# A two-layer hybrid encoder trunk: the streamed tile of the matmuls is read, and PSUM written, from the last column to the first

## The chip, the cores and the metric

The kernel runs on one core of one Trainium2 chip. The metric is device time in microseconds, the median of the runs of one kernel. "The span" is the time from the first to the last instruction of one profiled execution.

## What is computed

The reference is a trunk of two layers over x of 512 tokens by 2048 features, all in fp32. Cut to what matters:

```python
# layer 0
h = rmsnorm(x, a_norm);  proj = h @ a_w_in          # 2048 -> 2 x 2560
xb, gate = proj halves
xb = causal_depthwise_conv(xb)                      # width 4
r = sigmoid(block_diag(xb, w_r) + b_r); i = sigmoid(block_diag(xb, w_i) + b_i)   # 10 blocks of 256
log_a = -8 * r * softplus(-lam); a = exp(log_a)
y = scan(h = a * h + sqrt(1 - a*a) * i * xb)        # along the tokens
x = x + (y * silu(gate)) @ a_w_out                  # 2560 -> 2048
kv = rmsnorm(x, kv_norm) @ w_kv                     # 2048 -> 2 x 2048
# layer 1
proj = rmsnorm(x, b_norm) @ b_w_in                  # q and gate, 2048 each
o = stick_breaking_attention(q, k, v)               # 16 heads of 128, strictly causal
x = x + (o * silu(gate)) @ b_w_out
out = rmsnorm(x, final_norm)
```

## The kernel before

**Two parts for every operand.** TensorE works on fp32r tiles, a rounded form of fp32. To keep the accuracy, each operand is held as a high part (rounded) and a low part (the rest), and each product is three matmuls: high by high, high by low, low by high. `product` (line 355) issues them, and its one `pe.matmul` at line 359 is the line of nearly all matmuls in the profile. They add up in PSUM.

**Weights as the stationary side.** Activations are kept turned: features on the 128 partitions, the 512 tokens along the free axis. In most projections the weight block of 128 by 128 is the stationary operand and the turned activation tile, 128 by 512, is streamed; the result, 128 output features by 512 tokens, fills one PSUM bank of 512 fp32 words. That is `unit_t` (line 363): one unit is one loaded weight tile of 128 by 512, that is two blocks of rows by two blocks of columns, so four products, twelve matmuls, into two banks. `unit_t` is called by `unit1` (line 400, phase 1: the input projection from `x_hi`/`x_lo`, and the two gate matrices of the recurrence from `xc_hi`/`xc_lo`), in the loop of phase 2 (line 442: the output projection from `y_hi`/`y_lo`) and by `proj3` for j under 24 (line 448, phase 3: gate, q and k from `x_hi`/`x_lo`).

**The other matmuls.** In `proj3` from j = 24 on, v is computed with the activations as the stationary side and 256 weight columns streamed. `scores` and `values` do the attention, `turn_weights` (line 480) and `turn_x` (line 388) turn tiles with an identity, `unit4` and `last_columns` do the last projection with the attention output as the stationary side and 512 or 256 weight columns streamed, `add_x1` (line 535) adds the residual by a transpose, and `spread` (line 395) spreads the norm's factors over the partitions: a matmul on plain fp32 tiles, which the engine runs as two passes.

**What sets the order.** Weight tiles arrive from HBM through a ring of four stage slots. SyncE's queue loads a slot once its low part has been made (`lo_ready`). ScalarE makes the high part `w_hi` (lines 593 to 597) when the load has landed and TensorE has finished the unit that used the slot (`w_used`), VectorE makes the low part `w_lo` (lines 838 to 843), and TensorE waits for it at the head of each unit. The readers of the PSUM banks (VectorE, ScalarE) wait for `w_used` of the unit that ends a group; the semaphore is set by the last matmul of the unit. Their work is put by hand at fixed positions between the weight splits. GpSimd makes some of the low parts and masks. VectorE's cumulated products of the attention (line 1047) are scans that read and write `keep` and read `masked` from the last element to the first, and the scan of the recurrence (line 980) runs forward.

Phase 1 has 180 units, phase 2 has 80, and phase 3 has 256, of which 192 go through `unit_t`; the last projection has 64.

Of the kernel before, what the change touches and what calls it, by code (L numbers as in the profile page):

```python
# [32 lines left out]
P = 128  # L33
# [52 lines left out]
def build(nc, x, a_norm, a_w_in, a_conv_w, a_conv_b, a_w_r, a_b_r, a_w_i, a_b_i, a_lambda, a_w_out,  # L86
          kv_norm, w_kv, b_norm, b_w_in, b_w_out, final_norm, out):
    with ExitStack() as ctx:
        def sb(name, shape, dt=F32, scope=ctx):
            return scope.enter_context(nc.sbuf_tensor(name, shape, dt))  # L90
# [22 lines left out]
        w_hi = sb("w_hi", [P, RING, 512], F32R)  # L113
        w_lo = sb("w_lo", [P, RING, 512], F32R)
# [50 lines left out]
        ps = [ctx.enter_context(nc.psum_tensor(f"ps{b}", [P, S], F32)) for b in range(8)]  # L165
# [189 lines left out]
        def _(pe):  # L355
            def product(dst, a_hi, a_lo, b_hi, b_lo, start, stop, check=True):

                for n, (a, b) in enumerate(((a_hi, b_hi), (a_hi, b_lo), (a_lo, b_hi))):
                    mm = pe.matmul(dst, a, b, start=start and n == 0, stop=stop and n == 2,  # L359
                                   skip_group_check=not check)  # L360
                return mm

            def unit_t(j, u, bank, m_hi, m_lo, k0, k_end):

                pe.wait_ge(lo_ready, u + 1)
                s = j % RING
                for kk in range(2):
                    for m in range(2):
                        c = 256 * kk + P * m
                        mm = product(ps[bank + m][:, :], w_hi[:, s, c:c + P], w_lo[:, s, c:c + P],  # L370
                                     m_hi[:, k0 + kk, :], m_lo[:, k0 + kk, :],
                                     k0 + kk == 0, k0 + kk == k_end - 1)
                mm.then_inc(w_used, 1)

# [25 lines left out]
            def unit1(it, j):  # L400

                u = it * N1 + (U1 + j)
                b, jj = j // 18, j % 18
                if jj < 16:
                    unit_t(j, u, 2 * (jj // 8), x_hi, x_lo, 2 * (jj % 8), KD)
                else:
                    if jj == 16:
                        pe.wait_ge(xc_lo_ready, it * 4 + (2 * b + 2))
                    unit_t(j, u, 4 + 2 * (jj - 16), xc_hi, xc_lo, 0, 2)
# [27 lines left out]
            with pe.Fori(0, B2) as it:  # L437
                for j in range(N2):
                    jj = j % 10
                    if j < 10:  # L440
                        pe.wait_ge(y_lo_ready, 1 + 2 * jj + 2)
                    unit_t(j, it * N2 + (U2 + j), 2 * (j // 10), y_hi, y_lo, 2 * jj, KR)
# [53 lines left out]
            for j in range(TURN):  # L496
                if j < 8:
                    pe.wait_ge(x1_lo_ready, 2 * j + 2)
                if j == 6:

                    pe.wait_ge(acc_step, 2 + KD)
                    for t in range(TT):
                        mm = pe.matmul(ps[5][:, t:t + 1], acc[:, P * t:P * t + P], ones[:, 0:1],
                                       start=True, stop=True)
# [748 lines left out]
```

## Time and profile before

| what | value |
|---|---|
| median of 2 runs | 1705.97 us (1705.64 to 1706.29) |
| the profiled execution's own time | 1707.84 us |
| its span | 1706.1 us |
| TensorE busy | 1691.7 us (99%) |
| VectorE, ScalarE, GpSimd busy | 909.6, 798.0, 228.2 us |
| mean granted TensorE clock | 0.998 |
| DMA over the span | 95 GB/s |

PE is TensorE's matmul side and PEld its weight load, DVE is VectorE, ACT ScalarE, POOL GpSimd, SP SyncE. L359 is line 359 of the kernel. In a group, "ps<-x_hi,w_lo" names the output and the inputs, "128x512" the shape of the result, "x1408" the count, and behind the bar stand the busy time in us, the mean duration of one in ns, and the idle time of the engine before them with what ended it. A matmul's duration runs from its start to its modelled end, and those of neighbours overlap.

### The profile page before, as it was taken

To read this page: it belongs to the slowest core of one execution; us is meant where nothing else is said; L and a number is where in the kernel's file an instruction comes from. 1 tells how busy PE (TensorE), PEld (TensorE's weight loads), DVE (VectorE), ACT (ScalarE), POOL (GpSimd) and SP (SyncE) were. 2 spreads that over 40 slices of the span, in tenths; PEclk is the share of its full clock that TensorE was granted. 3 is DMA by queue.
4 is the path that set the end of the run, shared out by engine and by line. 5 is a ranking of instruction groups with operands and counts; after the bars stand their busy time and mean duration, and the time that the engine had idled before them with its cause. 6 is when DMAs were issued, how large, how long until landed. Compare 5 with 4: busy or idle time off the path is not lost.

```text
span 1706.1 us, 25540 instructions
## 1 busy us (share of the span) xinstructions
PE 1691.7 (99%) x8607; PEld 1448.8 (85%) x8607; DVE 909.6 (53%) x1688; ACT 798.0 (47%) x1622; POOL 228.2 (13%) x219
## 2 busy tenths in 40 slices
PE   8999999999999999999999999999999999999998
PEld 7888888888888888888889898988989898898888
DVE  5667676666675344354546455554645455453323
ACT  7655566666555233244445444453444444432223
POOL 0121221212212011021101010111101011112100
PEclk9999999999999999999999999999999999999999
DMA  5333333333333223223232322223232232323223
GB/s 182 99 105 94 98 97 93 91 98 97 100 99 99 94 97 98 92 89 98 75 98 79 90 83 86 86 80 92 81 92 80 86 92 75 98 74 112 93 94 135
DMA packets 155910, 162.22 MB, mean 95 GB/s; under 512 B 9608, under 2 KB 147032, under 8 KB 155736
## 3 DMA queue, kind: packets, MB, share of 16 engines
q1 hardware_dynamic: 155864, 161.63, 30.8%
q8 instruction: 26, 0.43, 0.1%
q14 instruction: 20, 0.16, 0.0%
HBM read 157.39 MB, written 4.19 MB: 95 GB/s over the span
## 4 chain that ended last, share of the span: by engine, by line
PE 98%; ACT 1%; DVE 0%; DMA 0%; issue 0%; POOL 0%; SPq 0%; POOLq 0%; DVEq 0%; ACTq 0%
PE ps L359 96%; PE ps L480 1%; PE ps L388 0%; PE ps L535 0%; DMA xraw<-in_x 0%; DVE rbuf L980 0%; POOL y_lo L1172 0%; ACT w_hi L593 0%; PE ps L395 0%; ACT abuf L677 0%; DVE w_lo L838 0%; DVE tbuf L976 0%; ACT L677 0%; ACT rbuf L665 0%; ACT tbuf L674 0%
## 5 line engine op out<-in xcount | busy, mean ns | idle before, releaser
L359 PE MATMUL ps<-x_hi,w_hi 128*128 128x512 f32 x1408 | 551.7, 392 | 0.0
L359 PE MATMUL ps<-x_hi,w_lo 128*128 128x512 f32 x1408 | 548.8, 390 | 0.0
L359 PE MATMUL ps<-x_lo,w_hi 128*128 128x512 f32 x1408 | 548.7, 390 | 0.0
L841 DVE SCALAR_TENSOR_TENSOR w_lo<-stage,cT,w_hi 128x256 fp32r<-128x256 f32 x416 | 230.5, 554 | 502.2 <-ACT w_hi L597 501.5
L595 ACT ACTIVATE w_hi<-stage,cT 128x256 fp32r<-128x256 f32 x416 | 211.1, 507 | 485.1 <-PE ps L359 484.9
L359 PEld LDWEIGHTS ps<-x_hi,w_lo 128*128 128x128 f32 x1408 | 264.7, 188 | 55.2
L359 PEld LDWEIGHTS ps<-x_hi,w_hi 128*128 128x128 f32 x1408 | 264.9, 188 | 54.5 <-issue 0.7
L359 PEld LDWEIGHTS ps<-x_lo,w_hi 128*128 128x128 f32 x1408 | 265.0, 188 | 54.4 <-issue 0.5
L838 DVE TENSOR_TENSOR w_lo<-stage,w_hi 128x512 fp32r<-128x512 f32 x160 | 129.0, 808 | 244.7 <-ACT w_hi L593 244.7
L593 ACT ACTIVATE w_hi<-stage 128x512 fp32r<-128x512 f32 x160 | 100.6, 631 | 266.8 <-PE ps L359 265.5
L843 DVE SCALAR_TENSOR_TENSOR w_lo<-stage,cT,w_hi 128x256 fp32r<-128x256 f32 x416 | 213.1, 512 | 0.0
L597 ACT ACTIVATE w_hi<-stage,cT 128x256 fp32r<-128x256 f32 x416 | 206.1, 495 | 0.0
L359 PE MATMUL ps<-w_hi,x_hi 128*128 128x256 f32 x512 | 145.6, 284 | 0.0
L359 PE MATMUL ps<-w_lo,x_hi 128*128 128x256 f32 x512 | 144.9, 283 | 0.0
L359 PE MATMUL ps<-w_hi,x_lo 128*128 128x256 f32 x512 | 144.9, 283 | 0.0
L359 PE MATMUL ps<-y_hi,w_hi 128*128 128x512 f32 x320 | 124.6, 389 | 0.7 <-POOL y_lo L1172 0.7
L359 PE MATMUL ps<-y_hi,w_lo 128*128 128x512 f32 x320 | 124.5, 389 | 0.0
L359 PE MATMUL ps<-y_lo,w_hi 128*128 128x512 f32 x320 | 124.5, 389 | 0.0
L359 PE MATMUL ps<-w_hi,o_hi 128*128 128x512 f32 (+1 forms) x288 | 103.5, 359 | 0.0
L359 PE MATMUL ps<-w_hi,o_lo 128*128 128x512 f32 (+1 forms) x288 | 102.0, 354 | 0.0
L359 PE MATMUL ps<-w_lo,o_hi 128*128 128x512 f32 (+1 forms) x288 | 101.9, 354 | 0.0
L359 PEld LDWEIGHTS ps<-w_lo,x_hi 128*128 128x128 f32 x512 | 97.4, 190 | 0.3
(161 smaller groups left out, 1994.4 us busy)
## 6 DMA issues: line engine op xcount, KB each, us to landing
stage<-in_a_w_in SPq DMA_DIRECT2D x160, 256.0 KB, 2.7
stage<-in_b_w_in SPq DMA_DIRECT2D x128, 256.0 KB, 2.6
stage<-in_w_kv SPq DMA_DIRECT2D x128, 256.0 KB, 2.6
stage<-in_a_w_out SPq DMA_DIRECT2D x80, 256.0 KB, 2.5
stage<-in_b_w_out SPq DMA_DIRECT2D x64, 256.0 KB, 3.1
out<-x SPq DMA_DIRECT2D x8, 512.0 KB, 3.2
xraw<-in_x SPq DMA_DIRECT2D x3, 1024.0 KB, 10.5
stage<-in_a_w_r SPq DMA_DIRECT2D x10, 256.0 KB, 2.9
```

The lines of the kernel that those rows point to most:

```text
L359: mm = pe.matmul(dst, a, b, start=start and n == 0, stop=stop and n == 2, skip_group_check=not check)
L480: mm = pe.transpose(ps[bank][:, c + P * (i - k):c + P * (i - k) + P], wgt[:, W_OFF[i] + P * k:W_OFF[i] + P * k + P], ident[:, :])
L593: nc.scalar.activation(w_hi[:, slot, :], stage[:, slot, :], ACT.Copy).then_inc(hi_ready, 1)
L595: nc.scalar.activation(w_hi[:, slot, 0:256], stage[:, slot, 0:256], ACT.Identity, scale=cT[:, col:col + 1])
L597: nc.scalar.activation(w_hi[:, slot, 256:512], stage[:, slot, 256:512], ACT.Identity, scale=cT[:, col + 1:col + 2]).then_inc(hi_ready, 1)
L838: nc.vector.tensor_tensor(w_lo[:, slot, :], stage[:, slot, :], f(w_hi[:, slot, :]), ALU.subtract).then_inc(lo_ready, 1)
L841: nc.vector.scalar_tensor_tensor(w_lo[:, slot, 0:256], stage[:, slot, 0:256], cT[:, col:col + 1], f(w_hi[:, slot, 0:256]), ALU.mult, ALU.s ...
L843: nc.vector.scalar_tensor_tensor(w_lo[:, slot, 256:512], stage[:, slot, 256:512], cT[:, col + 1:col + 2], f(w_hi[:, slot, 256:512]), ALU.m ...
```

## The change

In `unit_t`, the moving operands (high and low part) are taken with the free axis reversed, and so is the PSUM bank that they are written to. The step along the free axis goes from +1 to -1 on both, and the access starts at column 511 and ends at column 0. Stationary operands, counts, order of the instructions and semaphores are the same.

```diff
@@ -367,8 +367,8 @@
                 for kk in range(2):
                     for m in range(2):
                         c = 256 * kk + P * m
-                        mm = product(ps[bank + m][:, :], w_hi[:, s, c:c + P], w_lo[:, s, c:c + P],
-                                     m_hi[:, k0 + kk, :], m_lo[:, k0 + kk, :],
+                        mm = product(ps[bank + m][:, ::-1], w_hi[:, s, c:c + P], w_lo[:, s, c:c + P],
+                                     m_hi[:, k0 + kk, ::-1], m_lo[:, k0 + kk, ::-1],
                                      k0 + kk == 0, k0 + kk == k_end - 1)
                 mm.then_inc(w_used, 1)
```

## Rows read from the trace of the kernel before

**Rows 1.** The page: busy us, share of the span, instructions of each engine
```profile
PE 1691.7 (99%) x8607; PEld 1448.8 (85%) x8607; DVE 909.6 (53%) x1688; ACT 798.0 (47%) x1622; POOL 228.2 (13%) x219
```

**Rows 2.** The page: the chain that ended last, by engine and by line
```profile
PE 98%; ACT 1%; DVE 0%; DMA 0%; issue 0%; POOL 0%; SPq 0%; POOLq 0%; DVEq 0%; ACTq 0%
PE ps L359 96%; PE ps L480 1%; PE ps L388 0%; PE ps L535 0%; DMA xraw<-in_x 0%; DVE rbuf L980 0%; POOL y_lo L1172 0%; ACT w_hi L593 0%; PE ps L395 0%; ACT abuf L677 0%; DVE w_lo L838 0%; DVE tbuf L976 0%; ACT L677 0%; ACT rbuf L665 0%; ACT tbuf L674 0%
```

**Rows 3.** Waits: who waited for what, us in total, times, longest
```profile
DVE w_lo L841 <- ACT w_hi L597: 501.5, 275, 4.2
ACT w_hi L595 <- PE ps L359: 484.9, 284, 3.7
ACT w_hi L593 <- PE ps L359: 265.5, 127, 4.0
...
PE ps L388 <- DMA xraw<-in_x: 3.9, 2, 2.7
...
PE ps L377 <- DMA rows_g<-in_a_norm: 2.6, 1, 2.6
...
PE ps L359 <- POOL y_lo L1172: 0.7, 1, 0.7
```

**Rows 4.** Groups by form on TensorE: busy us, mean ns, idle before
```profile
L359 PE MATMUL ps<-x_hi,w_hi 128*128 128x512 f32 x1408 | 551.7, 392 | 0.0
...
L359 PE MATMUL ps<-y_hi,w_hi 128*128 128x512 f32 x320 | 124.6, 389 | 0.7 <-POOL y_lo L1172 0.7
...
L359 PE MATMUL ps<-xc_hi,w_hi 128*128 128x512 f32 x80 | 31.1, 389 | 0.0
```

**Rows 5.** The chain in order of time: start us, us, what
```profile
46.45 465.17 PE ps L359 x2052
...
1675.31 5.75 PE ps L359 x48
```

**Rows 6.** Timeline of TensorE and of its weight loads: start us, us, what
```profile
400.15 0.39 PE L359 MATMUL ps<-x_lo,w_hi 128*128 128x512 f32 x1
400.37 0.39 PE L359 MATMUL ps<-x_hi,w_lo 128*128 128x512 f32 x1
400.60 0.39 PE L359 MATMUL ps<-x_hi,w_hi 128*128 128x512 f32 x1
400.83 0.39 PE L359 MATMUL ps<-x_lo,w_hi 128*128 128x512 f32 x1
...
399.92 0.19 PEld L359 LDWEIGHTS ps<-x_lo,w_hi 128*128 128x128 f32 x1
400.15 0.19 PEld L359 LDWEIGHTS ps<-x_hi,w_lo 128*128 128x128 f32 x1
```

**Rows 7.** Three stretches: us, busy of PE, PEld, DVE, ACT, POOL; clock, DMA share, GB/s
```profile
46.45:511.60 465.15, 465.15 (x2053) 385.13 (x2053) 309.75 (x557) 274.30 (x511) 82.18 (x56) 1.00 0.33 97
534.10:743.80 209.70, 209.70 (x926) 173.64 (x927) 88.93 (x134) 67.23 (x117) 22.34 (x18) 1.00 0.30 96
756.50:1525.00 768.50, 768.50 (x4311) 676.50 (x4310) 403.10 (x780) 347.77 (x774) 93.35 (x114) 1.00 0.28 86
```

**Rows 8.** Around line 395: its weight loads, then the timeline of the loads behind it
```profile
L395 PEld LDWEIGHTS ps<-diag,ones x4: 187/190/192, 45.2 to 755.5; 128*128 128x128 f32 x4
...
45.20 0.42 PEld L395 LDWEIGHTS ps<-diag,ones 128*128 128x128 f32 x2
45.86 0.19 PEld L359 LDWEIGHTS ps<-x_hi,w_hi 128*128 128x128 f32 x1 [0.24 <-issue]
46.29 0.19 PEld L359 LDWEIGHTS ps<-x_lo,w_hi 128*128 128x128 f32 x1 [0.24 <-issue]
46.52 0.19 PEld L359 LDWEIGHTS ps<-x_hi,w_lo 128*128 128x128 f32 x1
```

**Rows 9.** Groups by form on VectorE: the scans
```profile
L1047 DVE TENSOR_TENSOR_SCAN keep<-keep,masked 128x512 f32<-128x512 f32 x16 | 23.7, 1480 | 0.0
L980 DVE TENSOR_TENSOR_SCAN rbuf<-abuf,tbuf 128x512 f32<-128x512 f32 x20 | 23.3, 1207 | 0.0
...
L1047 DVE TENSOR_TENSOR_SCAN keep<-keep,masked 128x384 f32<-128x384 f32 x16 | 15.0, 940 | 0.0
...
L1047 DVE TENSOR_TENSOR_SCAN keep<-keep,masked 128x256 f32<-128x256 f32 x16 | 10.5, 658 | 0.0
...
L1047 DVE TENSOR_TENSOR_SCAN keep<-keep,masked 128x128 f32<-128x128 f32 x16 | 6.6, 410 | 0.0
```

**Rows 10.** Timeline of VectorE around a reversed scan, and of GpSimd beside it
```profile
806.18 0.48 DVE L841 SCALAR_TENSOR_TENSOR w_lo<-stage,cT,w_hi 128x256 fp32r<-128x256 f32 x1 [3.91 <-ACT w_hi L597]
806.59 0.71 DVE L843 SCALAR_TENSOR_TENSOR w_lo<-stage,cT,w_hi 128x256 fp32r<-128x256 f32 x1
807.22 2.33 DVE L1047 TENSOR_TENSOR_SCAN keep<-keep,masked 128x512 f32<-128x512 f32 x2
...
810.52 0.47 DVE L841 SCALAR_TENSOR_TENSOR w_lo<-stage,cT,w_hi 128x256 fp32r<-128x256 f32 x1
...
806.55 1.07 POOL L1221 TENSOR_TENSOR wgt<-wgt,seen 128x128 f32<-128x128 f32 x2 [2.93 <-ACT wgt L733]
```

## The prediction

> **What bounds the kernel now.** I read the busy shares first. [rows 1] show TensorE busy 1691.7 of 1706.1 us, 99%, and the next engine, VectorE, at 53%. A busy share alone does not say that an engine sets the end, so the chain that ended last comes next: [rows 2] put 98% of it on PE and 96% on line 359, the one `matmul` call inside `product`. The waits [rows 3] close the case from the other side. VectorE waits 501.5 us for ScalarE's high parts of the weights, and ScalarE waits 484.9 and 265.5 us for TensorE to give stage slots back; TensorE's own waits are 3.9, 2.6 and 0.7 us. So every other engine runs at TensorE's pace, and the time is the number of matmuls times the distance between their starts, plus about 14 us at the two ends (1706.1 - 1691.7).
>
> That distance is not the "mean ns" of the groups. [rows 4] give a 128x512 matmul 389 to 392 ns, but those records overlap. The chain in order of time [rows 5] has 2052 of them in 465.17 us: 226.7 ns each, the same that neighbouring starts in the timeline show (400.15, 400.37, 400.60, 400.83) [rows 6]. The matmuls with 256 streamed columns stand in [rows 5] with 48 in 5.75 us: 119.8 ns each. The difference, 106.9 ns for 256 columns, is 0.418 ns a column, one cycle at the 2.4 GHz level, and the granted clock is 1.00 in every stretch [rows 7]. What is left, 226.7 - 512 x 0.418 = 12.9 ns, is a fixed part of each matmul. So the streamed operand enters at one column per cycle, and this rate is what the change touches: per column, one fp32 word is read per partition and one fp32 word is added into PSUM.
>
> **What the change touches.** Only `unit_t` changes. Its matmuls are the groups of [rows 4] with x, y or xc named as the input and 512 columns: 3 x 1408 for x, 3 x 320 for y, 3 x 80 for xc, together 5424 of the 8607 instructions in [rows 1]. At 226.7 ns they hold 1229.6 us, 72% of the span. The v projection, the scores, the values, the last projection and all transposes keep their order.
>
> **What goes away or is added, counted.** No instruction, wait, DMA or semaphore is added or removed. Both ends of each changed matmul are turned, so column c of the input still lands in column c of the bank: readers of the banks see the same layout, and since they wait for the last matmul of a unit, it does not matter to them that column 0 is now written last. All matmuls that add into one bank of a group are turned together, so two writes to the same word stay 512 columns apart, as before. The weights are read as before; a weight load's record is 188 to 192 ns and the next starts 227 ns after it [rows 6, 8], so it stays beside the stream. ScalarE, VectorE and the DMA queue do the same work at the pace that TensorE gives them. There is thus one term: 5424 times the change of the distance between starts.
>
> **Bounds for that term.** No TensorE row here has a step of -1, so I take the nearest rows from both sides.
>
> From below: 0 ns. The fastest streaming row in the trace is the present one, at a column per cycle of the full clock, and nothing in the order of addresses shortens that; the 12.9 ns fixed part, if all of it went, would be 70 us, but it is there for 256 and 512 columns alike and belongs to the instruction, not to its direction. I exclude a gain of more than a few microseconds. There are rows of backwards access, though on VectorE: the scans at line 1047 read `keep` and `masked` and write `keep` from the last element to the first. Their forms of 128, 256 and 384 elements take 410, 658 and 940 ns [rows 9], or (940 - 410) / 256 = 2.07 ns an element and 145 ns fixed. For 512 elements that gives 1205 ns, and the forward scan at line 980 takes 1207 ns [rows 9]. The backwards scan of 512 has a mean of 1480 ns, but in the timeline it begins at 807.22 while a GpSimd multiply runs from 806.55 to 807.62, and the weight split just before it, also under that multiply, shows 0.71 us where its neighbours show 0.47 to 0.48 [rows 10]. So the excess goes with GpSimd and not with the direction, and in SBUF both a read and a write of fp32 going down cost what they cost going up. The limit of this evidence is its rate: 2.07 ns an element is five times slower than TensorE's 0.418, it would hide a halved rate at the memory, and it says nothing of PSUM.
>
> From above: the trace has one 512-column stream at half the rate. The spread at line 395, on plain fp32 tiles and not fp32r ones, takes two passes of 512 columns. The weight loads behind it start at 45.86 and 46.29 [rows 8]: 0.43 us for a pass, two cycles a column. If a reversed stream loses the pairing of neighbouring words and moves one word per two cycles, each changed matmul goes from 0.2267 to 0.43 us, + 0.203; worked from the column price instead it is + 512 x 0.418 = + 0.214. Times 5424 that is + 1103 to + 1161 us. There is no cover: TensorE has 14 us of idle time in all, and its waits for x at the start are 3.9 us of that [rows 1, 3].
>
> I take the lower end, 0 ns. The words read and written are the same ones, and the same words are neighbours (511 with 510, 509 with 508); VectorE's rows show that a step of -1 is not handled as a jump; and the one slower stream in the trace goes with another data type and its two passes, not with an order of addresses. Both ends stay in the range, because no row shows PSUM written backwards at this rate.
>
> **A rule that speaks against the change.** The stream runs at one column per cycle [rows 5], and each column is a write into the bank. The Trainium skill, "Advanced Engine Details and Errata", section "PSUM Cachelines", says of 8-byte lines: "Any non-contiguous AP significantly slows down matmuls", and asks that every two consecutive elements be contiguous. Read strictly, a step of -1 is not contiguous and the rule makes this change a loss, of the size of the rival below; read as a rule on which words share a line, a descending pair fills a line as an ascending one does and the time stays. No run here decides between the readings. The section "SBUF Cachelines" of the same page asks for at least two hits on a 16-byte line, and a reversed fp32 stream has four; VectorE's equal prices [rows 9] agree with that at their slower rate.
>
> **The forecast.** Sum: the profiled span 1706.1 + 5424 x 0 = 1706.1 us. The profiled execution took 1707.84 us by its own time, 1.7 us more than its span, and the median of the unprofiled runs is 1705.97, within 0.2 us of the span. So I forecast 1706 us. A measurement of this kernel can tell about 2% (34 us) from no change; spread over 5424 matmuls 2% is only 6.3 ns each, so nearly any price per matmul would be seen.
>
> **Rivals.**
> 1. Half rate (the other side: much slower). Place: the stream of the 5424 matmuls, at the write of PSUM or the read of the moving tile. Mechanism: two neighbouring words go in one access only when the second address is above the first; descending, each word takes an access of its own. It decides as soon as the column takes over one cycle. Price as above: 1706 + 1103 to 1161, so 2809 to 2867 us, 2809 if the measured pass of line 395 is the model. For it: one column per cycle of full clock leaves no reserve, and half that rate exists in the trace. Against it: the rows of VectorE [rows 9], and that the same words stay neighbours.
> 2. A fixed price per matmul. The stream starts at the far end of the bank and of the tile, and a start costs once more what it costs now: 12.9 ns x 5424 = 70 us, 1776 us. For it: there is such a fixed part at all. Against it: it is the same for 256 and 512 columns, so it does not depend on where a stream ends, and nothing speaks for its depending on where it begins.
> 3. Worse than half: each word pays its own access, and matmuls no longer overlap their neighbours. If a start waited for the end of the one before, the distance would be the record's 390 ns plus the slower stream's 214, 0.604 us, that is + 0.377 x 5424 = + 2046, 3752 us. Only the absence of a row excludes it.
> 4. The change does nothing because both patterns are turned back to ascending before they reach the engine. The time would be the forecast's, 1706, and the trace could not tell it from the forecast; it is counted there.
>
> **How the numbers follow.** Same rate, cases 4 and forecast together: 0.58. Half rate: 0.29. A fixed price above 2%: 0.07. Worse than half: 0.04. A gain over 2%, for which I have no mechanism: 0.02. So faster 0.02, same 0.58, slower 0.29 + 0.07 + 0.04 = 0.40. The likeliest case's own range is 1701 to 1712 us. With the fixed price it holds 0.65, short of 0.8, so the range must reach to the half rate: 1700 to 2868 us. It holds 0.94 because the cases lie far apart and half rate cannot be taken in part.
>
> **What the profile of the changed kernel would show.** Right: line 359's groups with x, y and xc still near 390 ns and 226.7 ns apart, 2052 of them in about 465 us, PE busy 99%, VectorE and ScalarE waiting as now. Rival 1: starts 0.43 to 0.44 us apart only in the 512-column groups of `unit_t`, while the v projection stays at 119.8 ns and the scores and `unit4` at theirs; busy shares of VectorE and ScalarE fall to about 32 and 28%, their waits grow, DMA falls to some 57 GB/s. Rival 2: about 240 ns apart, the excess the same for each. The forecast is wrong if the start-to-start distance of these groups moves by over 6 ns; the granted clock of those stretches has to be read beside it, to tell a slower stream from a slower clock.

## The result and the profile after

The changed kernel takes 1741.98 us (1741.68 to 1742.28, 2 runs) against 1705.97 us before: a ratio of 1.0211, 95% interval 1.0167 to 1.0255. The profiled execution has a span of 1739.9 us, 33.8 us more than before.

The page of the changed kernel, busy shares, the chain by engine and by line, and the groups of the turned matmuls:

```profile
PE 1725.9 (99%) x8607; PEld 1449.6 (83%) x8607; DVE 904.4 (52%) x1688; ACT 799.1 (46%) x1622; POOL 226.5 (13%) x219
...
PE 99%; DMA 0%; ACT 0%; DVE 0%; SPq 0%; issue 0%
PE ps L359 97%; PE ps L480 1%; PE ps L388 0%; PE ps L535 0%; DMA xraw<-in_x 0%; PE ps L395 0%; ACT x L819 0%; PE ps L503 0%; ACT stage L814 0%; SPq L300 0%; SPq L277 0%; SPq L296 0%; DVE x L1120 0%; DVE rs_tok L861 0%; DVE small L859 0%
...
L359 PE MATMUL ps<-x_hi,w_hi 128*128 128x512 f32 x1408 | 562.6, 400 | 0.0
...
L359 PE MATMUL ps<-y_hi,w_hi 128*128 128x512 f32 x320 | 127.3, 398 | 0.1
```

Against [rows 1, 2, 4] nothing has changed its place. TensorE is still busy 99% of a longer span, the other engines have the same busy time (VectorE 904.4 for 909.6 us, ScalarE 799.1 for 798.0), and the record of a turned matmul is 8 to 9 ns longer. The distance between starts is in the chain in order of time (start us, us, what):

```profile
46.03 501.20 PE ps L359 x2148
...
1709.14 5.75 PE ps L359 x48
```

501.20 / 2148 is 233.3 ns, against 226.7 [rows 5]. The 48 matmuls of 256 columns that keep their order still take 5.75 us. The timeline shows the step in each start:

```profile
400.07 0.40 PE L359 MATMUL ps<-x_hi,w_hi 128*128 128x512 f32 x1
400.30 0.40 PE L359 MATMUL ps<-x_lo,w_hi 128*128 128x512 f32 x1
400.54 0.40 PE L359 MATMUL ps<-x_hi,w_lo 128*128 128x512 f32 x1
400.77 0.40 PE L359 MATMUL ps<-x_hi,w_hi 128*128 128x512 f32 x1
```

The granted clock is 1.00 in the same three stretches as in [rows 7]:

```profile
46.03:547.20 501.17, 501.17 (x2149) 403.48 (x2147) 319.64 (x574) 291.41 (x535) 86.99 (x61) 1.00 0.32 94
547.30:763.10 215.80, 215.80 (x926) 173.91 (x926) 87.56 (x134) 67.63 (x118) 21.70 (x18) 1.00 0.30 94
776.10:1558.00 781.90, 781.90 (x4306) 676.46 (x4305) 402.73 (x780) 346.67 (x773) 92.54 (x113) 1.00 0.28 84
```

So it is 16 cycles at the 2.4 GHz level, 6.67 ns, for each of 5424 matmuls: 36.2 us. The medians differ by 36.0 us. The two profiled spans differ by 33.8, because the profiled execution of before was 1.9 us slower than its median (1707.84 for 1705.97). Of the 2.4 us between 36.2 and 33.8, 0.7 us is the wait for `y_lo` [rows 3], which a slower TensorE no longer meets, and most of the remainder is at the very start: before the change eight distances of the first unit are 0.42 to 0.43 us, after it only two are. That is twice a normal distance, 512 columns at the 1.2 GHz level, although the profile's granted clock reads 1.00 there.

### The profile page after: what moved, and what is told of

The parts are those of the page before. It is cut to its first block, busy times and chain, and to the rows that moved or that the text cites. A ratio compares the mean times of both kernels' runs of the same rounds, so it can differ in the third digit from the quotient of the medians.

```text
span 1739.9 us, 25540 instructions
## 1 busy us (share of the span) xinstructions
PE 1725.9 (99%) x8607; PEld 1449.6 (83%) x8607; DVE 904.4 (52%) x1688; ACT 799.1 (46%) x1622; POOL 226.5 (13%) x219
## 4 chain that ended last, share of the span: by engine, by line
PE 99%; DMA 0%; ACT 0%; DVE 0%; SPq 0%; issue 0%
PE ps L359 97%; PE ps L480 1%; PE ps L388 0%; PE ps L535 0%; DMA xraw<-in_x 0%; PE ps L395 0%; ACT x L819 0%; PE ps L503 0%; ACT stage L814 0%; SPq L300 0%; SPq L277 0%; SPq L296 0%; DVE x L1120 0%; DVE rs_tok L861 0%; DVE small L859 0%
## 5 line engine op out<-in xcount | busy, mean ns | idle before, releaser
L359 PE MATMUL ps<-x_hi,w_hi 128*128 128x512 f32 x1408 | 562.6, 400 | 0.0
L359 PE MATMUL ps<-x_lo,w_hi 128*128 128x512 f32 x1408 | 559.8, 398 | 0.0
L359 PE MATMUL ps<-x_hi,w_lo 128*128 128x512 f32 x1408 | 559.7, 398 | 0.0
L838 DVE TENSOR_TENSOR w_lo<-stage,w_hi 128x512 fp32r<-128x512 f32 x160 | 123.3, 772 | 263.7 <-ACT w_hi L593 263.7
```

What stands on the lines that cost most here:

```text
L838: nc.vector.tensor_tensor(w_lo[:, slot, :], stage[:, slot, :], f(w_hi[:, slot, :]), ALU.subtract).then_inc(lo_ready, 1)
```

## The experiments

In all of them I read the distance between starts, forward 226.7 and turned 233.3 ns being the two known values. To try three orders in one kernel, the three phases get different ones: phase 1 streams x (and xc), phase 2 y, phase 3 x again. The chain's rows of these kernels are those of a stretch inside one phase. Each kernel from e5_lines to e11_offsets ran once, so its whole time is given but not reasoned from.

**Which side pays: e1_read and e2_write.** The changed kernel with one of its two edits undone.

```diff
 # e1_read
-mm = product(ps[bank + m][:, ::-1], w_hi[:, s, c:c + P], ...
+mm = product(ps[bank + m][:, :], w_hi[:, s, c:c + P], ...
 # e2_write
-             m_hi[:, k0 + kk, ::-1], m_lo[:, k0 + kk, ::-1],
+             m_hi[:, k0 + kk, :], m_lo[:, k0 + kk, :],
```

> Only the moving tiles are read from the last column to the first; PSUM is written forward, so the tokens come out in reversed order in each of these projections (what is computed is no longer the reference). Theory R (the 6.7 ns a matmul are paid on the read side of the reversed tile): starts 233.3 ns apart, 1742 us. Rival W (they are paid on the write side of PSUM): 226.7 ns, 1706 us. Rival B (half on each side): about 230 ns, 1724 us.

> Only the PSUM bank is written from the last column to the first; the tiles are read forward (tokens reversed again, not the reference's result). Theory R: 226.7 ns between starts, 1706 us. Rival W: 233.3 ns, 1742 us. Rival B: about 230 ns, 1724 us. If R and W both held with 233.3 ns in each of the two runs, the price would be paid once, whichever side turns.

Measured: reading turned 1742.36 us, 1.0214 (1.0184 to 1.0243); writing turned 1706.70 us, 0.9998 (0.9987 to 1.0010). The chain of the first, then of the second:

```profile
46.67 501.20 PE ps L359 x2148
```

```profile
45.34 465.17 PE ps L359 x2052
```

Theory R holds to the nanosecond: 233.3 ns and 226.7 ns. PSUM written from the last column to the first costs nothing; the whole price of this change is on the read of the streamed tile. The other orders tried below are put on both sides alike, so for them the two sides are not told apart.

**Fixed or per column: e3_v256 and e4_halves.** Both on top of the change.

```diff
 # e3_v256: the v projection, 256 columns
-mm = product(ps[2 + t // 2][:, 256 * (t % 2):256 * (t % 2) + 256], ...
+mm = product(bank[:, c + 255::-1] if c == 0 else bank[:, c + 255:c - 1:-1], ...
-             w_hi[:, s, 256 * kk:256 * kk + 256], w_lo[:, s, 256 * kk:256 * kk + 256],
+             back(w_hi, s, 256 * kk), back(w_lo, s, 256 * kk),
 # e4_halves: bank and tiles of unit_t
-[:, ::-1]
+[:, :].rearrange("p (h c) -> p h c", h=2)[:, :, ::-1]
```

> On top of the change, the v projection's 1536 matmuls of 256 columns are turned on both sides too. Theory fixed (one price per instruction): 119.8 + 6.7 = 126.5 ns between their starts, +10.2 us, 1752 us. Rival per column (one cycle more for every 32 columns): 119.8 + 3.3 = 123.1 ns, +5.1 us, 1747 us.

> Both sides are turned, but within each half of 256 columns (columns 255 to 0, then 511 to 256), so the pattern jumps once inside each of the 5424 matmuls. Theory fixed per instruction: 233.3 ns, 1742 us. Rival per turned stretch (each restart at a far end pays): 226.7 + 2 x 6.7 = 240.0 ns, 1778 us. Rival end of the tile (the price hangs on beginning at column 511): near 226.7 ns, 1706 us.

e3_v256: 1740.20 us, less than the changed kernel and not more. A pair of heads of phase 3 has two long stretches in the chain. First the changed kernel's, then those of e3_v256:

```profile
857.49 77.12 PE ps L359 x408
935.70 20.79 PE ps L359 x120
```

```profile
857.54 76.88 PE ps L359 x408
935.51 20.71 PE ps L359 x120
```

0.24 + 0.08 us are saved over the 192 matmuls of the v projection in a pair, 1.7 ns each. Both theories fall: at 256 columns a turned read does not cost less than at 512, it gains. e4_halves: 1742.90 us, 1.0217 (1.0187 to 1.0246), with the changed kernel's row:

```profile
46.94 501.20 PE ps L359 x2148
```

Turned within halves costs what turned as a whole costs, once per instruction, and beginning at column 511 is not the reason, since these streams begin at column 255.

**Which step downwards pays: e5_lines and e10_blocks.** The pattern is cut in blocks, on both sides.

```diff
 # e5_lines: phase 1, phase 2, phase 3
+ap.rearrange("p (b c) -> p b c", c=4)[:, :, ::-1]
+ap.rearrange("p (b c) -> p b c", c=4)[:, ::-1, :]
+for h in range(2): mm = product(dst[:, 256 * h:256 * h + 256], ...)
 # e10_blocks: phase 1, phase 2, phase 3
+ap.rearrange("p (b c) -> p b c", c=8)[:, :, ::-1]
+ap.rearrange("p (b c) -> p b c", c=16)[:, :, ::-1]
+ap.rearrange("p (b c) -> p b c", c=128)[:, :, ::-1]
```

> Three orders, one for each phase, on both sides of the matmul. Phase 1 goes up in blocks of four columns, each block from its last column to its first. Phase 2 goes down in blocks of four, each block forward. Phase 3 goes forward but as two matmuls of 256 columns in place of one of 512. Forward is 226.7 ns between starts, the changed kernel 233.3. Theory rate (a stream that goes down through memory runs a little slower for each column, by this table: 560 cycles for 512 columns and 284 for 256, against 544 and 287 forward): phase 1 stays at 226.7, phase 2 is at 233.3. Rival start (a fixed price for beginning at the last word of a group of four): phase 1 at 233.3, phase 2 at 226.7. Both: phase 3 at 119.8 ns a matmul, +30 us. If steps that are not of one piece cost far more, phases 1 and 2 go to 430 ns.

> Blocks that go up, each from its last column to its first, on both sides: of 8 columns in phase 1, of 16 in phase 2, of 128 in phase 3. So far blocks of 4 gave 226.7 ns and blocks of 32 gave 233.3. Theory shared read (what matters is where the stream is in memory beside the weight load, over stretches of tens of columns): the price grows with the block, 8 near 226.7, 16 between, 128 at 233.3. Rival piece (the stream is fetched in pieces of a fixed size, and only going down from piece to piece costs): 8 is at 226.7 or 233.3 and so are 16 and 128, with one jump and nothing between.

e5_lines takes 1753.94 us. A stretch of its phase 1 and one of its phase 2 in the chain:

```profile
59.89 340.23 PE ps L359 x1501
...
559.90 140.23 PE ps L359 x601
```

Columns 3, 2, 1, 0, 7, 6, 5, 4 and so on run at 340.23 / 1501 = 226.7 ns, and groups of four that go down, each of them forward, at 140.23 / 601 = 233.3. A group of four fp32 columns is 16 bytes. The order inside it is free and the order of the groups is what costs: theory rate as against start. The Trainium skill, "Advanced Engine Details and Errata", section "SBUF Cachelines", says that SBUF has 16-byte lines and that accesses which stay in one line run at full speed; phase 1, 226.7 ns, agrees with it. It says nothing of the order in which the lines come, and phase 2 shows that this order has a price.

e10_blocks takes 1771.95 us. The chain in its phases 1, 2 and 3:

```profile
59.99 240.10 PE ps L359 x1029
...
544.86 95.20 PE ps L359 x357
...
987.82 77.11 PE ps L359 x408
```

Blocks of 8 columns: 240.10 / 1029 = 233.3 ns. Blocks of 16: 95.20 / 357 = 266.7 ns, 40 ns over forward, the dearest order of all. Blocks of 128, in phase 3, give the changed kernel's 77.12 us for its stretch of 408, so 233.3 again, like blocks of 32 (below) and halves of 256. Neither theory has room for that: the price is not growing with the block and not one jump; blocks of 16 columns, 64 bytes, stand out alone. Whether their 40 ns are paid on the read or in PSUM was not tried.

**Widths, mixtures and other beginnings: e6_mix, e7_early, e8_v.**

```diff
 # e6_mix: phase 1
+pe.matmul(turned(dst, "back"), hi_w, turned(hi_m, "back"), ...)
+pe.matmul(dst, hi_w, lo_m, ...)
+mm = pe.matmul(turned(dst, "back"), lo_w, turned(hi_m, "back"), ...)
 # phase 2
+ap.rearrange("p (b c) -> p b c", c=256)[:, ::-1, :]
 # e7_early: phases 1 and 2 (there turned as well)
+first = 512 * (k0 + kk) - 1
+hi_m = m_hi.rearrange("p k c -> p (k c)")[:, first:first + 512]
 # e8_v: phase 1
+ap.rearrange("p (b c) -> p b c", c=32)[:, :, ::-1]
 # phase 2: columns 0 to 383, then 384 to 511, both turned; phase 3: v turned
```

> Phase 1: of the three matmuls of a product the two that stream the high part go down, the one that streams the low part goes up. Phase 2: the two halves of 256 columns are swapped, each of them forward. Phase 3: two matmuls of 256 columns, both going down. Theory rate: 235 ns in no place; phase 1 at 233.3, 233.3 and 226.7, mean 231.1; phase 2 at 226.7; phase 3 at 118.2 ns a matmul, as the turned v projection showed, +22 us. Rival start: phase 1 the same mean, phase 2 at 226.7, phase 3 at 119.8 + 6.7 = 126.5, +61 us. Rival tile (the price goes with the x and y tiles, the gain with the weight tiles): phase 3 at 123 or 126.5. Rival change of direction (what costs is the way from the end of one stream to the start of the next): phase 1 away from 231.1 either way.

> Phase 1 goes forward but the read begins one column early, at the last word of the tile before (all but the first k, so what is computed is shifted by a token there). Phase 2 the same piece of memory, read downwards, from column 510 to one before column 0. Phase 3 forward, split in 384 and 128 columns. Theory rate: phase 1 at 226.7, phase 2 at 233.3; phase 3: 416 cycles, 173.3 ns, for the matmul of 384. Rival start at the last word of a group of four: phase 1 at 233.3, phase 2 at 226.7. If crossing one group more costs, both are 0.4 to 0.8 ns longer.

> Phase 1 goes up in blocks of 32 columns, each block from its last column to its first. Phase 2 is split in 384 and 128 columns, both going down. Phase 3 is forward, with the v projection turned. Theory rate: phase 1 between 226.7 and 233.3 (16 changes of direction in place of one way down); phase 2's 384 columns at 422 cycles, 175.8 ns, against 173.3 forward, so the loss grows with the width and is a gain at 256; v at 118.2 ns, 1.6 ns less than forward, -2.5 us for all. Rival start: phase 1 at 233.3, phase 2's 384 columns at 173.3 + 6.7 = 180.0 ns.

e6_mix, 1758.12 us. In phase 1 each of the three matmuls has its own line, so the chain shows a product's period from one L390 to the next:

```profile
99.84 0.24 PE ps L390
100.08 0.23 PE ps L392
100.31 0.23 PE ps L393
100.54 0.24 PE ps L390
```

It is 0.70 us, a mean of 233.3 ns, as if all three were turned; 231.1 was expected, and only rival change of direction left room for another value. The three distances are not alike: 0.24 us from the first turned stream to the one that goes up (L392), then 0.23 and 0.23. The mixture costs what three turned streams cost, so the price is not a fixed sum for each instruction that goes down. Whether the changes of direction make the difference was not tried by themselves. Phase 2, halves swapped, is free, 140.08 / 618 = 226.7 ns, and so a jump backwards inside an instruction costs nothing:

```profile
559.95 140.08 PE ps L359 x618
```

Phase 3, two turned matmuls of 256 columns on the x tiles, has twelve starts in 1.42 us, 118.3 ns:

```profile
800.00 0.28 PE L359 MATMUL ps<-x_hi,w_hi 128*128 128x256 f32 x1
...
801.42 0.28 PE L359 MATMUL ps<-x_hi,w_hi 128*128 128x256 f32 x1
```

The same split going forward (e5_lines, phase 3) has twelve in 1.44 us, 120.0 ns:

```profile
799.89 0.28 PE L359 MATMUL ps<-x_hi,w_hi 128*128 128x256 f32 x1
...
801.33 0.28 PE L359 MATMUL ps<-x_hi,w_hi 128*128 128x256 f32 x1
```

So the gain at 256 columns goes with the width and not with the weight tiles: rival tile and rival start fall. (The whole times of e5_lines and e6_mix are 9 to 13 us longer than these distances make them, for the most part because with the split TensorE stands idle for some 1.5 us in each pass over two heads of phase 3, put down to "issue" in the chain.)

e7_early, 1869.00 us. A stretch of each of its phases 1 and 2 in the chain:

```profile
99.96 300.21 PE ps L359 x1313
...
559.86 140.27 PE ps L359 x586
```

A forward read that begins 4 bytes before its tile takes 300.21 / 1313 = 228.6 ns, and the same piece read downwards 140.27 / 586 = 239.4 ns, more than any whole turned tile. Neither number was foreseen; both are beyond the 0.4 to 0.8 ns of one more group. Phase 3, forward in 384 and 128 columns on the x tiles, was expected to show 173.3 ns behind a matmul of 384. Two starts that lie three rounds of six apart:

```profile
809.71 0.34 PE L359 MATMUL ps<-x_lo,w_hi 128*128 128x384 f32 x1
...
812.30 0.34 PE L359 MATMUL ps<-x_lo,w_hi 128*128 128x384 f32 x1
```

A round takes 2.59 / 3 = 0.863 us. Within it the starts are uneven (0.18 us behind two of the matmuls of 384, 0.23 behind the third), so no price of the 384 columns alone can be read.

e8_v, 1777.68 us. The chain in phase 1 and in a pair of heads of phase 3:

```profile
59.91 340.20 PE ps L359 x1458
...
908.66 75.29 PE ps L359 x408
```

Blocks of 32 columns cost the full price, 340.20 / 1458 = 233.3 ns. In phase 3 only the v projection is turned; the same stretch with all of it forward is in e2_write:

```profile
835.39 75.54 PE ps L359 x408
```

So the gain of 0.25 us in this stretch is there without any turned neighbour. The timeline of phase 2, the turned split in 384 and 128 columns:

```profile
599.75 0.34 PE L359 MATMUL ps<-y_lo,w_hi 128*128 128x384 f32 x1
599.92 0.34 PE L359 MATMUL ps<-y_hi,w_lo 128*128 128x384 f32 x1
600.11 0.22 PE L359 MATMUL ps<-y_hi,w_hi 128*128 128x128 f32 x1
...
600.62 0.34 PE L359 MATMUL ps<-y_lo,w_hi 128*128 128x384 f32 x1
...
602.35 0.34 PE L359 MATMUL ps<-y_lo,w_hi 128*128 128x384 f32 x1
```

The distances after two of the three matmuls of 384 columns are 0.17 and 0.19 us, and three rounds of six take 2.60 us (599.75 to 602.35), 0.867 us each, some 3 ns over the forward round of e7_early, which is on other tiles. Theory rate wanted 175.8 ns for each of 384 and rival start 180.0; the rhythm within a product is uneven and gives neither, so this phase decides nothing between them.

**Does the weight load take part: e9_narrow.**

```diff
+half = slice(0, 64)
+mm = product(turned(dst[half, :], how), hi_w[:, half], lo_w[:, half], turned(hi_m, how), ...)
```

> Phase 1: up in blocks of 64 columns, each block from its last column to its first. Phases 2 and 3: each product is done as two with 64 stationary columns each (both into the lower 64 partitions, so half of the result is not what it should be), phase 2 forward, phase 3 with both sides turned; so 2304 x 226.7 ns and 960 x 226.7 ns are added if the distance stays, about +740 us. Theory shared read (the part of each start-to-start distance over one cycle a column is time that the weight load's reads take from the stream's): half the weight columns, half the part: forward 512 + 16 cycles = 220.0 ns, turned 512 + 24 = 223.3 ns. Rival own start (the part belongs to the matmul's start, whatever its weights): 226.7 and 233.3 ns.

The kernel issues one narrow product for each of before, not two (the results for the other 64 weight columns are left out), so the counts stay and the 740 us of the text do not come: it takes 1738.72 us. The chain in phase 1 (blocks of 64), in phase 2 (forward, 64 weight columns) and in phase 3 (turned, 64 weight columns):

```profile
46.82 478.78 PE ps L359 x2052
...
559.81 180.31 PE ps L359 x784
...
779.80 20.30 PE ps L359 x87
```

Blocks of 64 columns cost 478.78 / 2052 = 233.3 ns. Forward with 64 weight columns takes 180.31 / 784 = 230.0 ns, slower than the 226.7 with 128 columns, and turned stays at 20.30 / 87 = 233.3. Shared read wanted 220.0 and 223.3, own start 226.7 and 233.3. The first falls as a count of stolen reads; but the second does not hold either, since the forward distance does change with 64 stationary columns. The edit also halves the PSUM partitions that are written, so it does not show that the weight load is the reason.

**Does the place in memory take part: e11_offsets.**

```diff
-w_lo = sb("w_lo", [P, RING, 512], F32R)
 x_hi = sb("x_hi", [P, KD, S], F32R)
+gap("before_w_lo", 32)
+w_lo = sb("w_lo", [P, RING, 512], F32R)
...
+gap("before_y_lo", 64, mem12)
 y_lo = sb("y_lo", [P, KR, S], F32R, mem12)
...
+unit_t(..., "forward" if jj < 8 else "back")     # phase 1; phase 2: j < 10
```

> So far every weight tile and every streamed tile began at a multiple of 2048 bytes in its partition. Here w_hi and x_hi still do; w_lo, x_lo and y_hi begin 32 bytes past one, y_lo 96. The groups of 8 (phase 1) or 10 (phase 2) units take turns: forward, then turned; phase 3 is turned. Theory beside (what costs is where the stream is relative to the weight load that runs beside it; the load of w_hi runs beside the first stream of a product, that of w_lo beside the second, on the low part): phase 1 keeps 226.7 ns forward, since low sits beside low with the same 32 bytes, and phase 2 leaves it, because y_hi's and y_lo's offsets differ from those of the loads. Rival own place (a stream pays for its own beginning within 64 or 128 bytes): the matmuls on the low part leave 226.7 already in phase 1. Rival neither (only going down costs): 226.7 and 233.3 everywhere, and a time near 1706 + 6.7 ns for each turned matmul.

1738.43 us. Stretches of the chain: turned and then forward in phase 1; turned, forward and forward in phase 2:

```profile
99.86 12.37 PE ps L361 x53
...
118.30 20.43 PE ps L361 x88
...
550.81 25.20 PE ps L361 x108
...
579.49 24.73 PE ps L361 x107
...
635.48 24.74 PE ps L361 x106
```

Forward is 20.43 / 88 = 232.2 ns in phase 1, and 24.73 / 107 = 231.1 and 24.74 / 106 = 233.4 in phase 2. Turned is 12.37 / 53 = 233.4 and 25.20 / 108 = 233.3, as with tiles at round addresses. So with some of the tiles 32 bytes off, forward streams lose nearly as much as turned ones: theory beside, which kept 226.7 in phase 1, falls, rival neither as well, and rival own place is right that phase 1 leaves 226.7. A stationary tile (w_lo) and a streamed one (x_lo) are moved together, so which of the two costs is not shown. The same code on the same addresses runs at 231.1 in one group of units and at 233.4 in a later one, which no sum of fixed prices for each instruction gives; it looks like a rhythm into which successive instructions settle.

The moved tiles also do at 256 columns what turning does. In a pair of heads of phase 3 the unit_t matmuls are turned as in e3_v256, but the v projection is forward, with w_lo and x_lo 32 bytes off:

```profile
855.39 76.80 PE ps L361 x408
```

That is 0.32 us less than the changed kernel's 77.12 and even a little less than the 76.88 with v turned; nine successive starts of the v projection span 0.94 us (914.79 to 915.73), 117.5 ns each, for 119.8 to 120.0 with nothing moved or turned. So the displacement loses at 512 columns and gains at 256, as the turn does. The two may be one effect; no run shows it.

**The version that the runs point to: e12_all256.** Forward for 512 columns, turned for 256.

```diff
+way = back if w == 256 else lambda ap: ap       # unit4
-mm = product(ps[t][:, 0:256], o_hi[...], o_lo[...],
-             hi_w[:, j % 4, c:c + 256], lo_w[:, j % 4, c:c + 256],
+mm = product(back(ps[t][:, 0:256]), o_hi[...], o_lo[...],
+             back(hi_w[:, j % 4, c:c + 256]), back(lo_w[:, j % 4, c:c + 256]),
```

> The kernel before, with only the matmuls of 256 streamed columns turned on both sides: 1536 of the v projection and 384 of the last quarter of the last projection (288 in the groups of the high part's weights, 96 beside them). At 118.3 ns in place of 119.8 to 120.0 that is 1.5 to 1.7 ns for each of 1920, so -2.9 to -3.3 us, ratio 0.998. Rival: the gain shows in the v projection only, -2.6 us, because the last columns read other tiles.

1702.95 us (11 runs) against 1706.95 for the kernel before, a ratio of 0.9982 (0.9973 to 0.9991); the expected 0.998 came. In the last projection 48 matmuls take 5.68 us for the 5.75 of [rows 5], 118.3 ns each, so the gain is not the v projection's alone:

```profile
1670.10 5.68 PE ps L359 x48
```

It is faster than the kernel before by some 0.2%, and than the changed one by 2.2%.

## Why the prediction was half right

- What bounds the kernel, the 5424 matmuls as the one term, the distance 226.7 ns and the absence of cover were right: 16 cycles on each are 36.2 us, and the medians differ by 36.0.
- The forecast itself failed. I put the change of that distance at 0 ns; it is 6.67. The stated test (wrong if the distance moves by over 6 ns) is met, and the loss of 2.1% sits just outside the 2% that the likeliest case stood for. The measured time is inside the range, but by its width and not by its mechanism: it was wide only because the half rate had to be in it, and the half rate did not come.
- The step that failed is the bound from below and the choice of its value. The argument was that the 12.9 ns beyond one cycle a column "belongs to the instruction, not to its direction" because 256 and 512 columns share it. Turned, they do not share it: it is 233.3 - 213.8 = 19.5 ns at 512 columns and 118.3 - 106.9 = 11.4 ns at 256. It depends on direction and width, and on where tiles begin (e11_offsets). The fast forward value is a favourable case (tiles at multiples of 2048 bytes, read upwards), not a floor that any order keeps. For the same reason "nothing in the order of addresses shortens that" was wrong at 256 columns.
- VectorE's rows did not bear on the question. I had written that their rate would hide a halved rate; it hides 16 cycles in 544 all the more. They were also read too kindly. The turned scan of 512 elements takes 1480 ns where 1205 was worked out, and that was put down to GpSimd, which runs beside its first 0.40 us. All 16 take 1478 to 1483 ns, and one of them has GpSimd beside its whole length (start us, us; then count, busy us, mean ns):

```profile
1515.78 1.97 POOL L1221 TENSOR_TENSOR wgt<-wgt,seen 128x128 f32<-128x128 f32 x2 [3.14 <-ACT wgt L733]
...
L1047 DVE TENSOR_TENSOR_SCAN keep<-keep,masked 128x512 f32<-128x512 f32 x1 | 1.5, 1482 | 0.0
```

  Nearly four times the overlap and the same time: that the excess goes with GpSimd is not shown, and equal prices in both directions hold only as far as the fit from the forms of 128 to 384 elements carries.
- Rival 2 named the right shape, a price of some nanoseconds for each matmul, at 0.07, and sized it at 12.9 ns (1776 us) because the present start cost was taken twice; 6.67 was measured. Its reason, the start at the far end, is not what the runs show: turned halves begin at column 255 and blocks of 8 at column 7, and both pay in full.
- Rival 1 is out on both sides. PSUM written downwards costs nothing (e2_write, 0.9998), so the strict reading of the Trainium skill's "Advanced Engine Details and Errata", section "PSUM Cachelines", does not hold for a step of -1. SBUF read downwards costs 3% of the distance and not 90%.

What stays open is the mechanism on the read side. Shown are: of the full turn only the read pays, the order inside 16 bytes is free, groups going down pay, a mixture pays in full, 64-byte blocks pay most, and a 32-byte shift of some tiles costs a forward stream almost as much. The number of stationary columns has some part (230.0 ns with 64), but that of the weight load was not isolated: no kernel here streams fp32r without loading weights.

## What to carry to other kernels

Where TensorE is 99% busy, the distance between starts is the number to watch, and a few cycles on each matmul are per cents of the whole; measure it from the chain's counts and not from the mean duration. Turning PSUM's side of a matmul was free here, so where an order must be turned, turn the write or the order inside groups of four columns. Full-width fp32r tiles at multiples of 2048 bytes, read upwards, were the fastest; for 256 columns a turned read is worth trying, 1.5 ns a matmul here.

## What was not expected of the hardware

- A streamed read that goes down takes 16 cycles more than one that goes up at 512 columns (233.3 for 226.7 ns) and about 4 fewer at 256 (118.3 for 119.8 to 120.0).
- Blocks of 16 columns, each backwards, take 266.7 ns, while blocks of 8, 32, 64, 128 and 256 take 233.3 and blocks of 4 take 226.7.
- With w_lo, x_lo and y_hi 32 bytes past a multiple of 2048 bytes, and y_lo 96, a forward stream of 512 columns goes from 226.7 to between 231.1 and 233.4 ns, and the forward v projection of 256 columns gets faster, 76.80 us for its stretch in place of 77.12.
- Two turned streams and a forward one in a product take 0.70 us, the same as with all three turned.
